# Linear attention: where weight parts, roots and unit order stand among scans, states and key spreads; a first gate by silu

## The reference, cut to what matters

```python
# first mixer: state-space part, gated by silu(z)
ssd_out = grouped_rmsnorm(y * jax.nn.silu(z), ssd_norm, SSD_GROUPS)

# linear attention (4 heads, key 128, value 256, chunks of 64)
bcum = jnp.cumsum(ac, axis=3); b_last = bcum[..., -1:, :]
q_dec = qc * jnp.exp(bcum); k_inv = kc * jnp.exp(-bcum); k_dec = kc * jnp.exp(b_last - bcum)
attn = jnp.where(causal, q_dec @ k_inv^T, 0.0); o_intra = attn @ vc
state = state * dec + kd^T @ vv            # per chunk; o_inter = qd @ state
o = rms_norm(o, o_gain); return (o * jax.nn.silu(z)) @ w_out

# delta rule (4 key heads, 8 value heads of 128)
q = l2_norm(q) * d ** -0.5; k = l2_norm(k)
gc = jnp.cumsum(g); decay = exp(gc_i - gc_j) where causal
tri = where(strict, (kb @ k^T) * decay, 0) + I
u = solve(tri, vb); w = solve(tri, kb * exp(gc))
```

## Time and profile before

| | |
|---|---|
| runs | 1384.17, 1385.26, 1379.89 us (median 1384.17) |
| profiled execution | 1376.87 us, of which the span 1375.1 |
| mean granted TensorE clock | 0.928 |
| PE busy | 1124.3 us, 82% |
| DVE busy | 634.5 us, 46% |
| ACT busy | 430.6 us, 31% |
| DMA, mean over the span | 227 GB/s |

### The profile page before, as it was taken

One profiled execution on the slowest core, in us unless ns is written; L12 is line 12 of the kernel. 1 busy time (PEld: TensorE's weight loads), 2 busy tenths in 40 slices (PEclk: granted clock), 3 DMA queues, 4 the chain that ended last, 5 costly groups with the idle time before them and its releaser, 6 DMA issues.

```text
span 1375.1 us, 20033 instructions
## 1 busy us (share of the span) xinstructions
PE 1124.3 (82%) x8294; PEld 842.4 (61%) x8294; DVE 634.5 (46%) x1251; ACT 430.6 (31%) x665; POOL 6.1 (0%) x28
## 2 busy tenths in 40 slices
PE   4999998786655656566567999998899979799998
PEld 4999877532121212122126988796679978689887
DVE  4777487510101011010106458756567946564586
ACT  3554344100000000000005435545345652255353
POOL 1000000000000000000000000000000000000000
PEclk9999999898887888888888999999999999999999
DMA  8385315799999999999999653244233520055400
GB/s 280 125 255 184 123 62 197 309 397 409 409 410 410 409 410 410 410 410 410 410 409 294 158 160 114 97 158 172 73 122 124 184 62 3 1 151 176 160 4 31
DMA packets 119654, 312.57 MB, mean 227 GB/s; under 512 B 17059, under 2 KB 17290, under 8 KB 119578
## 3 DMA queue, kind: packets, MB, share of 16 engines
q1 hardware_dynamic: 116864, 310.78, 61.6%
q10 hardware_dynamic: 2714, 0.71, 0.2%
HBM read 310.42 MB, written 1.05 MB: 227 GB/s over the span
## 4 chain that ended last, share of the span: by engine, by line
PE 61%; DMA 26%; DVE 7%; ACT 3%; issue 2%; SPq 1%; ACTq 0%; DVEq 0%
DMA ring<-in_w_up 17%; DMA ring<-in_w_down 8%; PE bank L2133 8%; PE bank L2137 8%; PE bank L2140 7%; PE bank L2151 6%; PE bank L2158 6%; PE bank L2155 5%; PE bank L2396 4%; PE bank L2417 2%; PE bank L2196 2%; DVE w_l L1140 1%; PE bank L2075 1%; PE bank L2215 1%; PE bank L2385 1%
## 5 line engine op out<-in xcount | busy, mean ns | idle before, releaser
L1140 DVE TENSOR_TENSOR w_l<-ring,w_h 128x1024 fp32r<-128x1024 f32 x204 | 246.5, 1222 | 112.2 <-ACT w_h L649 110.2
L649 ACT ACTIVATE w_h<-ring 128x1024 fp32r<-128x1024 f32 x204 | 214.2, 1057 | 234.0 <-PE bank L2140 126.8
L2396 PE MATMUL bank<-ring,cm 128*32 128x512 f32 x960 | 148.3, 750 | 113.1 <-DMA ring<-in_w_up 64.5
L2396 PEld LDWEIGHTS bank<-ring,cm 128*32 128x32 f32 x960 | 29.2, 127 | 226.9 <-DMA ring<-in_w_up 94.0
L2133 PE MATMUL bank<-hnT_h,w_h 128*128 128x256 f32 x864 | 125.1, 288 | 2.8 <-ACT w_h L649 1.8
L2137 PE MATMUL bank<-hnT_l,w_h 128*128 128x256 f32 x864 | 122.8, 285 | 0.0
L2140 PE MATMUL bank<-hnT_h,w_l 128*128 128x256 f32 x864 | 121.9, 284 | 0.0
L2133 PEld LDWEIGHTS bank<-hnT_h,w_h 128*128 128x128 f32 x864 | 112.6, 193 | 6.2 <-issue 2.9
L2137 PEld LDWEIGHTS bank<-hnT_l,w_h 128*128 128x128 f32 x864 | 113.0, 194 | 0.0
L2140 PEld LDWEIGHTS bank<-hnT_h,w_l 128*128 128x128 f32 x864 | 112.1, 193 | 0.4 <-DVE w_l L1140 0.4
L2417 PE MATMUL bank<-ring,cm 128*32 128x512 f32 x496 | 72.1, 722 | 44.2 <-DMA ring<-in_w_down 39.4
(11 more groups left out here) (418 smaller groups left out, 1328.9 us busy)
## 6 DMA issues: line engine op xcount, KB each, us to landing
ring<-in_w_down SPq DMA_DIRECT2D x62, 1024.0 KB, 15.8
ring<-in_w_gate SPq DMA_DIRECT2D x60, 1024.0 KB, 14.9
ring<-in_w_up SPq DMA_DIRECT2D x60, 1024.0 KB, 15.8
ring<-in_fox_w_in SPq DMA_DIRECT2D x32, 1024.0 KB, 10.6
ring<-in_w_in SPq DMA_DIRECT2D x22, 1024.0 KB, 9.2
ring<-in_gla_w_in SPq DMA_DIRECT2D x12, 1024.0 KB, 6.3
ring<-in_gdn_w_in SPq DMA_DIRECT2D x12, 1024.0 KB, 6.7
ring<-in_w_out SPq DMA_DIRECT2D x8, 1024.0 KB, 6.3
```

The costliest lines, as they stand in the source:

```text
L649: af(part(w_h, u, width), w, ACT.Copy).then_inc(s["high_ready"], 1)
L1140: v.tensor_tensor(part(w_l, u, width), w, part(w_h, u, width).bitcast(F32), ALU.subtract).then_inc(s["low_ready"], 1)
L2396: x = mm(bank[a][CAP * e:CAP * (e + 1), :], m_xg[:, 2 * b + r, CAP * e:CAP * (e + 1)], expert_of(w, e)[:, r * FF:(r + 1) * FF], start=(b = ...
```

## The change

Four edits, none of which adds a transfer:

- Linear layer: DVE's `low` between the scans may go up to unit `3 * UNITS + 2`, so units 11, 12 and 13 stand there. ACT makes the exponentials in the order 20, 28, 24 with no `high` between them (unit 15's high part is made by the next `copy_bank`). DVE multiplies the keys with tile 28 after the second exponential and waits for the third only ahead of the product with tile 24.
- Linear layer: `out_roots` of the first 128 tokens stands ahead of the third state's wait.
- Delta layer: the last unit of block 5 is multiplied first, and all four spread pairs come behind it. `decays` is cut in two: `falls` (the spread decays, which count a new semaphore `gdn_fall`, on which ACT now waits) and `products` (which count `gdn_bc`, as before). `gdn_qk_ready` is waited for between the first falls and the first products. DVE makes mask and delta of one half before those of the other, for chunk 0.
- First gate: the last four banks of the projection are copied with silu at scale 1; the tanhs, the DVE products and their semaphores go. The first gated product waits for the projection's copies.

```diff
@@ ACT, state-space layer
-                copy_bank("ssd", 6 + b, cmf[:, dst[b] * T:(dst[b] + 2) * T], 0.5 if b >= 12 else 1.0)
+                copy_bank("ssd", 6 + b, cmf[:, dst[b] * T:(dst[b] + 2) * T], 1.0, ACT.Silu if b >= 12 else ACT.Copy)
...
-                if i == 1:
-                    silu_z(0, 2)
...
-                act.wait_ge(s["z_ready"], 2)
@@ ACT, linear layer
                         decay_exp(20, 16, 1.0)
-                        high(n + 16)
+                        decay_exp(28, 28, 1.0)
                         decay_exp(24, 16, -1.0)
-                        decay_exp(28, 28, 1.0)
@@ ACT, delta layer
-                    act.wait_ge(s["gdn_bc"], 2 * c + hf + 1)
+                    act.wait_ge(s["gdn_fall"], 2 * c + hf + 1)
@@ DVE, state-space layer
-                if i == 3:
-                    silu_z("ssd", 0)
                 if i == 6:
+                    dve.wait_ge(s["proj_copied"], 22)
                     gated(0)
@@ DVE, linear layer
-                        low(min(n_low[0] + 1, UNIT_BASE["gla"] + 3 * UNITS))
+                        low(min(n_low[0] + 1, UNIT_BASE["gla"] + 3 * UNITS + 2))
...
                 low(n + 14)
-                dve.wait_ge(s["gla_exp"], 3)
+                dve.wait_ge(s["gla_exp"], 2)
                 link(v.tensor_tensor(tf(28, 4), tf(4, 4), tf(28, 4), ALU.mult))
                 low(n + 15)
+                dve.wait_ge(s["gla_exp"], 3)
                 v.tensor_tensor(tf(4, 4), tf(4, 4), tf(24, 4), ALU.mult).then_inc(s["gla_qk"], 1)
...
                 for c in range(3):
+                    if c == 2:
+                        out_roots("gla", GLA_H, 0, 1.0 / GLA_DV)
                     dve.wait_ge(s["gla_st"], c + 1)
...
-                out_roots("gla", GLA_H, 0, 1.0 / GLA_DV)
                 low(n + 5 * UNITS + 6)
@@ DVE, delta layer
                 for hf in (0, 1):
                     masked(0, hf)
-                for hf in (0, 1):
                     delta(0, hf)
@@ PE, delta layer
-                project("gdn", 5, 6, lambda m: m >= 2 and spread("gdn_qk", 8, lambda i: [i], (0, 1) if m == 2 else (2, 3)))
+                project("gdn", 5, 6)
+                spread("gdn_qk", 8, lambda i: [i])
                 pe.wait_ge(s["gdn_conv_done"], 4)
                 pe.wait_ge(s["proj_copied"], PROJ_BASE["gdn"] + 12)
-                pe.wait_ge(s["gdn_qk_ready"], 1)
...
-                def decays(c, hf):
+                def falls(c, hf):
+                    for j in range(4):
+                        x = mm(b4(g_fall[hf])[:, j, :], row_of(4 * hf + j, P), fall[:, c * P:(c + 1) * P], start=True, stop=True)
+                    x.then_inc(s["gdn_fall"], 1)
+
+                def products(c, hf):
                     cc = slice(c * P, (c + 1) * P)
-                    for j in range(4):
-                        mm(b4(g_fall[hf])[:, j, :], row_of(4 * hf + j, P), fall[:, cc], start=True, stop=True)
...
-                decays(0, 0)
-                decays(0, 1)
+                falls(0, 0)
+                pe.wait_ge(s["gdn_qk_ready"], 1)
+                products(0, 0)
+                falls(0, 1)
+                products(0, 1)
                 halves(0)
                 for hf in (0, 1):
-                    decays(1, hf)
+                    falls(1, hf)
+                    products(1, hf)
```

More of the change, by code:

```diff
@@ L117 @@
 ROW_TURN = {"ssd": 1, "gdn": 2}
-Z_USE = {"ssd": 0}
 O_USE = {"gla": 0, "gdn": 1}
@@ L281, in build @@
             "out_high", "out_low", "ssd_added",
-            "lin_ready", "z_tanh", "z_ready",
+            "lin_ready",
             "row_arg", "qk_ready", "row_ln", "row_ready", "row_turned", "col_ready",
@@ L299, in build @@
             "gdn_row_free", "gdn_beta_exp", "gdn_last", "gdn_col_step", "gdn_conv_done", "gdn_qk_ready",
-            "gdn_xt", "gdn_xtc", "gdn_kt", "gdn_ktc", "gdn_bc", "gdn_arg", "gdn_exp", "gdn_masked", "gdn_tap", "gdn_x", "gdn_turned", "gdn_q_ready",
+            "gdn_xt", "gdn_xtc", "gdn_kt", "gdn_ktc", "gdn_fall", "gdn_bc", "gdn_arg", "gdn_exp", "gdn_masked", "gdn_tap", "gdn_x", "gdn_turned", "gdn_q_ready",
             "gdn_qt_ready", "gdn_power", "gdn_r", "gdn_r_ready", "gdn_uw", "gdn_u_ready", "gdn_w_ready", "gdn_state",
@@ L755, in squares @@
                 af(sq[:, g % 2].rearrange("p a b -> p (a b)"), src, ACT.Square).then_inc(s["sq_ready"], 1)
[L757 to L762, removed]
             def softplus_row(k, src, dst, parts):
@@ L1295, in add_projection @@
                     x_lows(following, (2, 3))
[L1297 to L1306, removed]
             def conv(src, dst, weights, stride, taps, bias=None, units=0, first=None):
```

## The result

The changed kernel takes 1367.51 us (median of 6 runs, 1364.17 to 1372.21) against 1381.12 for the kernel before in the same comparison (6 runs, 1379.38 to 1385.26): a ratio of 0.9892, 95% interval 0.9874 to 0.9911, 13.6 us faster. The forecast was a gain of 10.8 us, to 1373.4. Measured twice more against before, the same kernel gave 0.9845 [0.9828, 0.9862] and 0.9902 [0.9872, 0.9933]. Over all its 19 executions the mean is 1365.9, that of 75 executions of before 1382.1: 16.2 us, with a standard deviation of 4.1 us for one execution of the changed kernel and 2.7 for one of before. What may make the changed kernel scatter more is taken up under the explanation.

The account below looks back on a forecast made before the run. The prediction took TensorE to hold most of the bounding chain, DMA about a quarter, so edits gain only from TensorE's waits. Terms 3.1 + 1.2 + 6.1 + 0.4 = 10.8 us off 1384.17 gave 1373.4 us, range 1366.5 to 1381.0.

Parts of the forecast that it names:

- gate: State-space layer: without tanhs and DVE gate products, TensorE's 0.39 us wait goes; 0.4 us gained, bounds 0 and 0.4.
- scans: Linear layer: low parts made among the scans start unit 16 earlier; 3.1 us gained, bounds 1.8 and 5.7.
- roots, to the delta layer: Linear layer's end: first roots ahead of the last state copy bring output products earlier; 1.2 us gained, bounds 0 and 2.0.
- delta, to the first triangle turn: Delta layer: last unit before the spreads and earlier falls bring the triangle turn to 1115.5; 5.8 us gained.
- delta, second chunk: Delta layer: ACT starts behind the falls too, but its copies of the first powers limit this; 0.3 us more.
- the 2.2: Linear layer's scans: TensorE would still wait 2.2 us, until 941.8, for unit 14's low part.
- I take 3.1, because a wait of 1.75 was followed by the 0.50 clock: Linear layer's scans: chose the gain with the low clock still following the shorter wait, 3.1 us rather than 5.7.
- The stated upper bound, 5.7: Linear layer's scans: 5.7 us gained if the shorter wait leaves the clock at 1.00.
- The clock stays up: Rival, 12%: no clock fall where waits shrink to about 2.2 us; 14.9 us gained in all, 1369.3.
- Its other half, 1.5 in the delta layer: Delta-layer share of the 12% rival in which shrunken waits no longer bring the clock down: 1.5 us more gained.
- The cover: Linear layer's end: DVE's free 3.96 us before the last state holds the first roots' 3.48, so nothing is delayed.
- the next thing is late then: Linear layer's end: the turn also waits for ACT's last gate silu at 995.96, limiting the gain to 1.2 us.

Follow-up runs that it names:

- e7: The changed kernel with the old first gate (half scale, tanh, two DVE products); 0.9907 against before, 1367.37 us.
- e9: The changed kernel as it is, timed once more beside three other versions; 0.9902 against before, 1367.41 us.
- e10: The kernel before with 24 idle identity products filling TensorE's 5.31 us wait ahead of unit 12's low third; 1.0009 against before.
- e5: The kernel before with the silu gate alone; 0.9996 against before.
- e13: The changed kernel with the last gate unit's first four products moved ahead of the wait for the linear layer's third state; 0.9894 against before, 1366.62 us.

## Why the forecast was right in kind and too small

By stretches of the profiles, with the edit against without it:

| term | forecast | without | with | gained |
|---|---|---|---|---|
| gate | 0.4 | 56.29 to 56.32 (3 profiles) | 55.82 to 55.86 (7) | 0.5 |
| scans | 3.1 | 57.5 mean (57.16 to 57.70, 5) | 51.69 to 51.73 (6; 53.29 in e7) | 5.8 |
| roots, to the delta layer | 1.2 | 77.2 mean (76.6 to 77.9, 6) | 74.8 mean (73.0 to 76.2, 9) | 2.4 |
| delta, to the first triangle turn | 5.8 | 81.4 mean (80.5 to 82.3, 6) | 76.5 (11, all within 0.02) | 4.9 |
| delta, second chunk | 0.3 | 47.97 at its shortest | 47.74 at its shortest | 0.2 |

The sum is 13.8. The last row compares the shortest; by means it is 50.9 (48.0 to 54.0, 6) against 49.6 (47.7 to 51.2, 11), 1.3 with a scatter larger than that, and the sum would be 14.9. By the medians of the three comparisons the gain is 13.6, 20.9 and 14.8. The second lies far from the others. Its one profile (span 1366.7) shows no stretch that the others lack; e9's, in which the clock falls at none of the places below, took 1358.96, so the executions of 1360 to 1363 in that comparison can be such ones, but none of them was profiled.

The absolute forecast, 1373.4, lies 5.9 above the 1367.51 measured. Of that, 3.1 is the base: the forecast was taken off 1384.17, the median of three runs, and six runs gave 1381.12. The other 2.8 is the gain, 13.6 instead of 10.8, and there the scans' term is the one that was mis-sized most: 3.1 said, 5.8 measured.

**Scans: the choice between two ends was wrong.** Up to the wait all steps held: the order, the hidden table load, the 2.2. The step that failed is "I take 3.1, because a wait of 1.75 was followed by the 0.50 clock". Behind 2.20 us the clock stayed at 1.00 in six profiles and fell in one. The stated upper bound, 5.7, is what was measured. Even the execution with a fall (e7) gains 4.2, since its fall costs 1.6, where the one behind 5.31 us costs 2.2 (e10), a price that 3.1 carried over whole and put at 2.6. The argument from one row (1.75, then 0.50) treated the fall as fixed by the wait's length. It isn't: 1.81 was followed by 1.94 in one execution of a kernel and by 3.68 in another. The Trainium skill (TensorE: Matmul & The Clock Gate, Part 1: The HAM clock gate) says that how many slow products a kernel shows at its start varies from run to run. The pairs here, 1.94 against 3.68 behind 1.81 us, show the same variation in a kernel's middle. So the rival "The clock stays up" described this place rightly, with 2.6 us more. Its other half, 1.5 in the delta layer, held in some executions only (below).

**Roots: the sizes of what comes next were read from a slow stretch.** The cover held (the first roots end before the state copy is due). Then the working said that ACT is late next, with its silu at 994.70 and its square at 991.02. Both times were rows of an execution in which the clock was at 0.50 around 990, and before the change it did not matter, since DVE's two sets of roots in a row set the turn: 35.54 to 35.56 in all six profiles without the edit, with or without a fall. With DVE's chain halved, ACT's and TensorE's times do matter, and they are shorter when the clock is up. So up to the first turn the term is 2.6 at full clock (35.55 to 32.95, where the hole before the turn is put down to DVE), 0.2 with the longest fall (35.36, ACT), and 1.0 to 1.5 in five profiles between them. The stretch behind the turn brings the rest of the table's mean. 1.2 was a fair reading of one case and not of the mean. The step that failed here is "the next thing is late then", with ACT's silu done at 995.96: at full clock ACT isn't what the turn waits for (e9: 1.85, put down to DVE).

**Delta layer: right to 0.2 in its own execution, somewhat large for the mean.** The steps came out nearly to the tenth: spreads at full pace, the second falls' 0.26, the wait before the turn from 3.14 to 2.25, the first powers' wait from 1.40 to 1.18. From the profile of before, 82.15 to 76.51 is 5.6, where 5.8 was said. But the 3.67 for the first spreads is itself the slow clock; in three other profiles of the old order the same products take 2.05 behind the same wait or a longer one (2.06 and 2.41), and the stretch is 80.5 to 80.9. After the change it is the same in all eleven.

**Gate: right.** 0.5 against 0.4, by the stretches alone; e5's time can't show it. No table load of its own appeared in the stretch with silus. The Trainium skill (ScalarE: Activation LUTs, What ACT_TABLE_LOAD costs) counts a drain of 1.38 us on top of the load; here the load at 1101.24 took 1.28, the activation before it had ended at 1101.22, and the next one began at 1102.54, so the trace bears out the load and shows no drain.

**The scatter.** Where the clock fell decides several us of an execution. Of the changed kernel's places, two are in the linear layer: the last state product (2.4) and the turn behind it (up to 1.5). In the old order a fall at the first of them left the turn where it was (35.54 to 35.56), so it adds scatter only after the change; that this makes the 4.1 against 2.7 isn't shown. A third is the wait of 2.25 before the triangle turn, or the end of the inversion behind it. From that turn to the first state it is 47.74 us in the three profiles in which the clock stays at 1.00 throughout, 49.2 to 49.3 in the three where it falls at the triangle turn, and 50.2 to 51.2 in the five where it falls at the inversion's end. That last fall runs on behind the first state: up to the second forget layer's small products it is 122.5 to 122.7, 124.0 to 124.2 and 126.4 to 127.0 us for the three kinds, so it costs about 4 us. So the 1.5 of the rival is real, in eight executions of eleven by one fall or the other not collected. Sixteen products at the inversion's end, in the changed kernel's first profile and then in e9:

```profile
1155.47 3.78 PE L2713 MATMUL bank<-vtm,hnT 128*128 128x128 f32 x16
```

```profile
1148.47 2.05 PE L2713 MATMUL bank<-vtm,hnT 128*128 128x128 f32 x16
```

No edit touches them, and in the 8 us ahead of them no wait is longer than 0.7 us. The waits there are the same in both profiles (0.63, 0.22, 0.68, 0.21), and so is TensorE's busy time in 3 us of it, at the same distance from the triangle turn, first in the changed kernel's first profile and then in e9:

```profile
1150.00:1153.00 3.00, 2.11 (x49) 1.86 (x45) 2.78 (x6) 0.18 (x1) 0.00 (x0) 1.00 0.00 0
```

```profile
1143.73:1146.73 3.00, 2.11 (x49) 1.86 (x45) 2.78 (x6) 0.18 (x1) 0.00 (x0) 1.00 0.00 0
```

Whether fillers there would hold the clock up wasn't tried.

## What to carry to other kernels

When a wait on TensorE shrinks to a few microseconds, give the term two values, with and without the clock's fall, and a chance to each; one execution's fall is no rule for the next, so look whether durations in the row come from a slow stretch before using them. A stretch between two fixed instructions sizes an edit to tenths where whole times leave 2 to 4 us. And work moved into a hole leaves its old place empty: in e13's profile the clock stayed up in the filled hole and fell in the next.

## What the hardware showed unexpectedly

The granted clock after an idle TensorE isn't set by the idle time alone: 1.00 behind 2.20 us (six profiles), 0.50 behind 2.20 (one); with a wait of 1.81 before the last state product, a fall in the wait or in the product in six profiles and none in three; and 0.50 at the inversion's end in five profiles of eleven, behind stretches in which TensorE is busy 2.1 of 3.0 us in small products and no wait exceeds 0.7 us; e9 has the same stretch and stays at 1.00. A slow clock can also be free: in the kernel before, keeping it up gave 2.2 us and half of it went to the wait that came next. And the last part of the kernel, from the second forget layer's small products on, takes 129.1 or 130.8 us, in kernels with and without every edit: 1.7 us of scatter that no edit here made.
